# One opening and one product order of a diffusion layer: adaLN by column quarters, S5 preparation inside it, paired context matmuls

## The reference

```python
ml = split(silu(c) @ ada_w + ada_b, 9)         # shift, scale, gate x 3 sub-layers; mc likewise from c_ctx
x   = ffn_sublayer(x,   ml[0], ml[1], ml[2], ffn1_norm, w_gate, w_up, w_down)     # first feed-forward
ctx = ffn_sublayer(ctx, mc[0], mc[1], mc[2], ffn1_norm, w_gate, w_up, w_down)
# ... token mixing: S5 branch and gated linear attention branch on modulate(rms_norm(.), ml[3], ml[4])
x = x + ml[5] * y_lat
x = ffn_sublayer(x, ml[6], ml[7], ml[8], ffn2_norm, ...)                          # second one, latents only
return rms_norm(x, final_norm)

def ffn_sublayer(t, shift, scale, gate, norm_g, w_gate, w_up, w_down):
    h = rms_norm(t, norm_g) * (1 + scale) + shift
    return t + gate * (0.5 * ((silu(h @ w_gate) * (h @ w_up)) @ w_down))
```

## Time and profile before

| | |
|---|---|
| runs, device time | 1355.12, 1355.15, 1356.28 us; median 1355.15 |
| span of the profiled execution | 1354.2 us |
| busy share of the span | PE 98%, PEld 91%, DVE 64%, POOL 48%, ACT 30% |
| chain that ended last, by engine | PE 93%, DVE 3%, DMA 2%, SP's queue 1% |
| first real product of the feed-forward | 40.94 us into the span |

### The profile page before, as it was taken

How to read it: one execution, slowest core, us unless ns; L and a number is a source line. 1 busy time by engine, 2 the same in 40 slices (tenths; PEclk the granted TensorE clock), 3 DMA queues, 4 the chain that set the end, 5 groups by cost and what they waited for, 6 DMA issues and landing times.

```text
span 1354.2 us, 21460 instructions
## 1 busy us (share of the span) xinstructions
PE 1333.5 (98%) x8546; PEld 1229.7 (91%) x8546; DVE 865.3 (64%) x1376; ACT 400.0 (30%) x757; POOL 651.0 (48%) x408
## 2 busy tenths in 40 slices
PE   5999999999999999999999999999999999999998
PEld 4899999999999999998888888888998999999997
DVE  5787368568556555437656649826778765555666
ACT  4320010210210110124635321222142555544455
POOL 1544444543543533532732356636467455655554
PEclk9999999999999999999999999999999999999999
DMA  9553354353444344223322479484736233344322
GB/s 357 161 148 85 121 148 120 120 157 116 126 135 139 102 126 158 62 55 109 80 62 52 126 212 259 152 266 148 229 87 199 63 94 94 107 115 114 101 72 85
DMA packets 236782, 178.18 MB, mean 132 GB/s; under 512 B 33416, under 2 KB 211852, under 8 KB 236684
## 3 DMA queue, kind: packets, MB, share of 16 engines
q1 hardware_dynamic: 216624, 145.78, 37.6%
q10 hardware_dynamic: 20060, 31.04, 7.0%
HBM read 156.93 MB, written 19.86 MB: 131 GB/s over the span
## 4 chain that ended last, share of the span: by engine, by line
PE 93%; DVE 3%; DMA 2%; SPq 1%; issue 1%; ACT 0%; DVEq 0%; ACTq 0%
PE ps L1244 47%; PE ps L1971 13%; PE ps L1566 13%; PE ps L2030 7%; DMA ada_w<-in_ada_w_dram 2%; PE ps L1255 1%; PE ps L1844 1%; DVE ada_acc L2860 1%; DVE ps L2972 1%; PE ps L2057 1%; PE ps L1881 1%; PE ps L1669 1%; PE ps L1487 1%; PE ps L1438 1%; PE ps L1706 1%
## 5 line engine op out<-in xcount | busy, mean ns | idle before, releaser
L1143 POOL TENSOR_SCALAR w_hi<-w_raw 128x1024 fp32r<-128x1024 f32 x128 | 153.4, 1198 | 527.8 <-PE ps L1244 276.0
L1146 POOL TENSOR_TENSOR w_lo<-w_raw,w_hi 128x1024 fp32r<-128x1024 f32 x128 | 325.4, 2542 | 10.7
L1244 PE MATMUL ps<-h_hi,w_lo 128*128 128x384 f32 (+2 forms) x1000 | 291.4, 351 | 0.0
L1244 PE MATMUL ps<-h_hi,w_hi 128*128 128x384 f32 (+2 forms) x1000 | 287.1, 346 | 0.0
L1244 PE MATMUL ps<-h_lo,w_hi 128*128 128x384 f32 (+2 forms) x1000 | 287.0, 346 | 0.0
L1244 PEld LDWEIGHTS ps<-h_hi,w_lo 128*128 128x128 f32 x1000 | 178.8, 188 | 14.9 <-issue 4.3
L1244 PEld LDWEIGHTS ps<-h_lo,w_hi 128*128 128x128 f32 x1000 | 180.6, 188 | 10.5
L1244 PEld LDWEIGHTS ps<-h_hi,w_hi 128*128 128x128 f32 x1000 | 180.4, 188 | 10.7
L1222 POOL TENSOR_TENSOR w_lo<-w_raw,w_hi 128x512 fp32r<-128x512 f32 x90 | 115.6, 1297 | 105.7 <-ACT w_hi L2609 104.2
L2860 DVE SCALAR_TENSOR_TENSOR ada_acc<-ada_w,cs,ada_acc 128x1024 f32<-128x1024 f32 x70 | 108.3, 1581 | 7.8 <-DMA ada_w<-in_ada_w_dram 5.5
L1971 PE MATMUL ps<-h_hi,w_hi 128*128 128x256 f32 x360 | 102.0, 283 | 0.0
(11 more groups left out here) (459 smaller groups left out, 2635.0 us busy)
## 6 DMA issues: line engine op xcount, KB each, us to landing
w_raw<-in_ffn_w_gate_dram SPq DMA_DIRECT2D x44, 512.0 KB, 5.1
w_raw<-in_ffn_w_up_dram SPq DMA_DIRECT2D x44, 512.0 KB, 4.1
w_raw<-in_ffn_w_down_dram SPq DMA_DIRECT2D x44, 512.0 KB, 4.5
ada_w<-in_ada_w_dram ACTq DMA_DIRECT2D x32, 512.0 KB, 3.9
w_raw<-in_w_in_dram SPq DMA_DIRECT2D x32, 512.0 KB, 4.3
ada_w<-in_ada_w_dram SPq DMA_DIRECT2D x30, 512.0 KB, 4.3
c_scr<-cp ACTq DMA_DIRECT2D x16, 288.0 KB, 3.8
b_scr<-bt_sb ACTq DMA_DIRECT2D x16, 256.0 KB, 3.9
```

The source lines that it names most:

```text
L1143: pool.tensor_scalar(w_hi[:, s, 0:cols], w_raw[:, s, 0:cols], 1.0, 1.0, ALU.mult, ALU.mult)\
L1146: pool.tensor_tensor(w_lo[:, s, 0:cols], w_raw[:, s, 0:cols], w_hi[:, s, 0:cols].bitcast(F32), ALU.subtract).then_inc(w_split, 1)
L1244: last = pe.matmul(mv[2], st, mv[part], start=(first and q == 0), stop=(n == len(terms) - 1 and q == 2))
```

## The change

**Opening.** x is turned token tile by token tile. adaLN's groups 1 and 0 come in four quarters of 256 columns, 1 MB for each group and quarter in one transfer (rows of 1 KB). For each quarter PE does 8 matmuls for each group (L1324 of the changed kernel) and four of 2 columns that turn the rows (L1336, by `strip_eye`); DVE then has what it needs for k = 2q and 2q+1 of h. Quarter 0 stands before the feed-forward, quarters 1 to 3 stand between joint steps, which now are of three jobs, v=0 to 2. x times rstd is made first, and scale and shift come in one DVE instruction for latents and one for context; ACT's copy of that is `h_hi`. The loads are in the order unit 0, unit 1, quarter 0, unit 2, quarter 1, and quarters 2 and 3 when a buffer is free.

**S5 preparation.** On DVE `s5_angle` stands between quarters 0 and 1, `s5_roots` between quarters 2 and 3, and `s5_powers` behind the two first `ada_add` and ahead of the first product.

**Pairs.** The high and low parts of h and of the activations lie side by side. A k-step of the first feed-forward is five matmuls: w_hi times context high and low side by side (512 columns) into the context bank, w_lo times context high (256) into its first half, and three of 512 columns for the latents. DVE adds the two halves of the context bank (`sum_halves`) before the gate's silu and before the product; the gate's slot is given back after that. The sums for adaLN's group 2 and later stand in other banks.

```diff
-            for k in range(KD):
-                sp.dma_start(first_tile(1, k), ada_src(1, k)).then_inc(ada_here0[1][k], 16)
...
-            for k in range(KD):
-                sp.dma_start(first_tile(0, k), ada_src(0, k)).then_inc(ada_here0[0][k], 16)
...
+            first_unit(0)
+            first_unit(1)
+            quarter(0)
+            first_unit(2)
+            quarter(1)
+            sp.wait_ge(row_made, 2)
+            quarter(2)
+            sp.wait_ge(row_made, 3)
+            quarter(3)
...
+                    def pair_step(j, wh, wl, hi, lo, pair, first, final, between=None):
...
+                        mm(None, ctx_(j), wh, pair, first, False)
+                        mm(0, ctx_half(j, 0), wl, hi[:, NL:NT], False, final)
+                        mm(None, lat(j), wl, hi[:, 0:NL], first, False)
+                        mm(1, lat(j), wh, lo[:, 0:NL], False, False)
+                        return mm(2, lat(j), wh, hi[:, 0:NL], False, final)
...
+                    if joint:
+                        joint_start(0)
+                        joint_start(1)
+                        joint_step((0, 1), 0)
+                        joint_step((0, 1), 1)
+                        row_products(1, 1)
+                        row_products(1, 0)
+                        joint_start(2)
+                        joint_step((2,), 0)
+                        turn_rows(1)
+                        joint_step((2,), 1)
+                        joint_step((0,), 2)
+                        row_products(2, 1)
...
-                        act.wait_ge(job_done, (jg + 1) + i * part.jseg)
                         if n == NT:
-                            dst, src = dst.rearrange("p (b c) -> p b c", b=2), both(jg, 384)
+                            act.activation(dst[:, 0:NL], src, ACT.Silu)
+                            act.wait_ge(gate_summed, i * SEG + (part.segs * SEG + f + 1))
+                            dst, src = dst[:, NL:NT], half_sum[:, 0, :]
                         act.activation(dst, src, ACT.Silu).then_inc(slot_read[jg % 4], 1)
...
+                        if n == NT:
+                            done(jg)
+                            sum_halves(jg, 0).then_inc(gate_summed, 1)
...
-                            if f_ == 2:
-                                s5_roots()
-                            if f_ == 3:
-                                s5_powers()
...
+            s5_angle()
+            quarter_mod(1)
+            quarter_low(1)
+            quarter_mod(2)
+            quarter_low(2)
+            s5_roots()
+            quarter_mod(3)
+            quarter_low(3)
...
             for k in range(2):
                 ada_add(ADA_START, k)
-            s5_angle()
+            s5_powers()
             ffn(JOB["ffn1"], PARTS1, NT, 0, 0)
...
+            def sum_halves(j, n):
+
+                return dve.tensor_reduce(half_sum[:, n, :], ctx_(j).rearrange("p (h c) -> p c h", h=2), AX.X, ALU.add)
```

More of the change, by code:

```diff
@@ L184 @@
 STRIP = 32
-JOINT_FROM = 2
+JOINT = 3
 def ada_acc0(g):
@@ L660, in both, with tokens, ctx_half @@
         return ps[:, 2 * (j % 4):2 * (j % 4) + 2, 0:n]
[L662 to L666, removed]
+    def tokens(j):
+        return ps[:, 2 * (j % 4):2 * (j % 4) + 2, :].rearrange("p b c -> p (b c)")[:, 0:NT]
+    def ctx_half(j, part):
+        return ctx_(j)[:, NC * part:NC * part + NC]
     def ada_cols(j, c0=0):
@@ L1269, in _, with turn_vecs @@
                 last.then_inc(job_done, 1)
[L1271 to L1283, removed]
-                    if g == 0 and k < KD - 1:
-                        keep_busy(2)
+            def turn_vecs():
+                j = JOB["vec"]
+                wait_read(pe, j)
+                pe.wait_ge(vec_in, 16 * 9)
+                transpose(lat(j)[:, 0:P], vecs[:, :]).then_inc(job_done, 1)
@@ new lines, in row_products @@
+            def row_products(q, g):
+                j = JOB["open"]
+                if q or not g:
+                    pe.wait_ge(row_ok, q + (q > 0 or g == 0))
+                pe.wait_ge(ada_here0[g][q], 16)
+                for k in range(KD):
+                    r = STRIP * (k % 4)
+                    last = pe.matmul(lat(j)[r:r + STRIP, QW * g:QW * g + QW], cs_wide[:, k, :], quarter_tile(g, q)[:, k, :],
+                                     start=(k < 4), stop=(k >= 4))
+                if g == 0 or q == 0:
+                    last.then_inc(row_made, 1)
@@ new lines, in turn_rows @@
+            def turn_rows(q, groups=(1, 0)):
+                j = JOB["open"]
+                pe.wait_ge(row_ok, q + 2 - (q == 0 and groups == (1,)))
+                for g in groups:
+                    for c in range(2):
+                        at = 8 * q + 4 * g + 2 * c
+                        last = pe.matmul(ctx_(j)[:, at:at + 2], ada_row[:, q % 2, QW * g + P * c:QW * g + P * c + P], strip_eye[:, 0:2],
+                                         start=True, stop=True)
+                if q < QUARTERS - 1:
+                    last.then_inc(cols_made, 1)
+                else:
+                    last.then_inc(job_done, 1)
@@ L1479, in slot_free, with mm, pair_job @@
                         pe.wait_ge(slot_read[j % 4], j // 4 + i * (part.jseg // 4))
-                    joint = 2 if two and part.segs + i == 0 else 0
+                    def pair_step(j, wh, wl, hi, lo, pair, first, final, between=None):
+                        def mm(q, o, st, mv, start, stop):
+                            ins = pe.matmul(o, st, mv, start=start, stop=stop)
+                            if between and q is not None:
+                                between(q)
+                            return ins
+                        mm(None, ctx_(j), wh, pair, first, False)
[3 more added lines that the diff above has]
+                        return mm(2, lat(j), wh, hi[:, 0:NL], False, final)
+                    def pair_job(j, wh, wl, between=None):
+                        for k in range(KD):
+                            last = pair_step(j, wh[:, k, :], wl[:, k, :], h_hi[:, k, :], h_lo[:, k, :], h_pair[:, :, k, NL:NT], k == 0, k == KD - 1,
+                                             (lambda r: between(k, r)) if between else None)
+                        return last
+                    joint = JOINT if two and part.segs + i == 0 else 0
                     def joint_hi(v, k):
@@ L1492, in joint_lo @@
                         wh = wv((u0 + v) % 4, KD, P)[0]
-                        for q in range(2):
-                            last = pe.matmul((lat, ctx_)[q](js.gu(v))[:, 0:384], wh[:, k, :],
-                                             h_lo[:, k, 384 * q:384 * q + 384], start=False, stop=(k == KD - 1))
+                        pe.matmul(lat(js.gu(v)), wh[:, k, :], h_lo[:, k, 0:NL], start=False, stop=(k == KD - 1))
+                        last = pe.matmul(ctx_half(js.gu(v), 1), wh[:, k, :], h_lo[:, k, NL:NT], start=False, stop=(k == KD - 1))
```

423 lines of the change are left out of this document (230 added, 193 removed).

## The result

The changed kernel takes 1391.13 us (median of four runs, 1389.13 to 1392.46) against 1355.13: a ratio of 1.0261, 95% interval 1.0246 to 1.0276. It is 36 us slower, where no measurable change was forecast and 1361 was the range's upper end. Its profiled span is 1390.7 us.

A forecast was written before the change was run, and what follows sets the result against it. PE, busy 1333.5 of 1354.2 us, was taken as the bound. Terms 0 + 2.2 + 0.5 − 0.2 − 2.8 + 0.5 = +0.2 gave a span of 1354.4, written as 1355.4 us measured; range 1347.5 to 1361.

The forecast's parts named there:

- The first product starts near 25.3: Opening: the first feed-forward product starts near 25.3 us, some 15.6 us sooner than the 40.94 before.
- the end of the joint steps, 60.9: Opening: three joint jobs, with row products, turns, a wait and slow clock between, end at 60.9 us, against 66.9 before.
- the turns: Opening: turning the rows between the joint steps takes about 0.8 us in all.
- PE's lead: After the three joint jobs PE is 6.0 us ahead of the kernel before, v=3 ending at 69.2 against 75.2.
- The wait at v=4: Segment 0: s5_powers, sum_halves and silu hold v=4 until 75.2; PE waits 6.0 us, term 0 (−6.0 to +0.9).
- the forecast's upper bound: s5_powers beside POOL's splits: one DVE instruction for each POOL instruction, ending at 75.3, so v=4 starts at 76.1.
- The clock behind the wait at v=4: +0.5: Segment 0: a lower granted clock after v=4's wait costs +0.5 us (0 to 1.7).
- PE waits inside v=7: I take 2.2 (0 to 4.6): Segment 0: adaLN adds some 4 us later make v=7's sums wait, 2.2 us (0 to 4.6).
- Two reductions, a split product and a split down add some 1.4 us of DVE per tile: Side segments: DVE's added 1.4 us per tile is nearly covered by its 1.52 us of idle time.
- the term was +0.5 for all: Side segments: lost cover costs 0.1 to 0.5 us at each of five segments' ends, +0.5 us (0 to 2.5).
- Pairs: −2.8 us: Paired k-steps: 6.3 ns less each (0 to 13) over 448 steps outside v=3 to 7, −2.8 us (−6.0 to 0).
- The lock also holds the adds: Rival: adaLN adds slow too, last near 107, v=7's sums wait 5 us; +4.4, 1359.6 us; chance 0.22.

The follow-up runs named there:

- without fillers: Changed kernel without paired products, s5_powers behind the fourth product again, and 23 of 27 filler matmuls left out of the opening: 1355.20 us, ratio 0.9998.
- The run with the opening and nothing lost behind it: Changed kernel without the paired products and with s5_powers behind the fourth product of segment 0 again: 1354.77 us, ratio 0.9996 to the kernel before.
- the powers back: Changed kernel with one edit, s5_powers behind the fourth product of segment 0 again, as in the kernel before: 1379.66 us, ratio 1.0174.
- one bank: The kernel with both edits, with the context's products of every k-step but the first written into the latents' bank: 1365.98 us, one execution.
- one piece: The kernel with both edits, with the pair's 512 columns read from one SBUF piece, the latents' high part: 1359.17 us, one execution.
- the kernel with both edits: Changed kernel with s5_powers behind the fourth product again and the up job's context sum kept in PSUM: 1366.88 us, ratio 1.0083.
- the run without pairs: Changed kernel without the paired products; the new opening and s5_powers ahead of the first product stay: 1367.67 us, ratio 1.0092.
- the run with later sums: The kernel with both edits, with v=7's adaLN sums two at a place from the sixth k-step, not one from the third: 1356.21 us, ratio 1.0008.

## Why the prediction was wrong

**The opening's end: right in kind, 6 us off.** "The first product starts near 25.3" was 29.42, and the end of the joint steps, 60.9, was 66.60. The transfers were not what held the start: PE went through fillers without a gap, behind the statistics of x; without fillers the start was 27.15. Inside the joint steps, the turns were priced at 0.8 us in all and took 0.80 for each of three, from the row at 36.79 to the next product at 37.59. So PE's lead was 0.1 us at the end of v=3, not 6.0. The run with the opening and nothing lost behind it, 1354.77 us with its first product at 30.50, shows that a first product 10.4 us sooner is worth nothing here: three quarters of the row products, which stood ahead of the first product, now stand behind it on PE's path.

**The wait at v=4: the mechanism as forecast, the place late.** The chain named (powers, `sum_halves`, silu, slot) is what the rows show. Since there was no lead to eat, the 4.61 us of wait were all lost. The powers also passed more slowly: the six of 256 columns took 66.36 to 77.5, one for each POOL instruction, the forecast's upper bound. (They are 21 instructions in all, not 22, which changes 0.25 us.) Here the rule of the Trainium skill, "SBUF — State Buffer", section "Who interferes with whom", was nearer than the pace I took from narrower instructions.

**A step that failed: "The clock behind the wait at v=4: +0.5".** I priced no clock behind the wait in v=7 at all. The half clock cost about 2.4 us at v=4 (half of 79.70 to 84.50) and 8.4 in v=7, and stretches of the same length at half clock (17.49 to 17.85 us, where 9.5 is the time at full clock) came in four other kernels. Moving the sums three k-steps back, by which nothing is computed sooner, returned 10.7 us, where the wait had been 2.42.

**"PE waits inside v=7: I take 2.2 (0 to 4.6)".** 4.28 was inside, but through another door: not only the last add but the fourth gate's sum behind it. I had looked for slots that wait on DVE at v=4 and in the side segments, and not at this one.

**The step that failed most: "Two reductions, a split product and a split down add some 1.4 us of DVE per tile".** It is 0.69 + 0.69 + 0.70 + 2.15 less the old 0.96, 3.3 us, and the 1.52 us of idle time did not cover it: +11.4 in the two segments that have most adds, none in the other two, where the term was +0.5 for all. One operand moved back to PSUM returned 13.7 us, the most of any single edit. The rule on two SBUF operands (the Trainium skill, "SBUF — State Buffer", section "Who interferes with whom"), which I had cited for `s5_powers`, I did not apply to the product that the change made into one. The trace agrees with it: 2151 ns against 422 with one operand in PSUM.

**"Pairs: −2.8 us".** The mechanism was right and the term mis-sized: a k-step is 3 ns shorter, not 6.3. The two side segments without waits are 0.05 us shorter each.

**The rivals.** "The lock also holds the adds" came nearest: the last add did end after 102.3 (at 112.77). Its price was only 4.4 us: it held 5.9 of waits and 1.0 more, where 10.9 us of half clock and the slow product came on top of the waits.

## What to carry to other kernels

Before a reduction or a copy moves an operand from PSUM to SBUF, list what the instruction behind it now reads: with both operands in SBUF it ran here at the pace of a busy POOL, and most slowly right where the freed buffer lets POOL start. A wait on a PE that was full cost its length and, in all but one trace of v=7's wait, the clock behind it: price it from a stretch of the same profile at either level, and where a few small matmuls need a late result, put them as late as they can stand. An earlier start is worth only what is not moved from a waiting PE into a full one.

## What the runs showed of the chip

Behind waits of nearly one length in the same place of v=7, the granted clock fell at once and stayed at 0.50 for 17.85 us (a wait of 2.42), fell only some 2 us later (2.34 with the powers back, 2.40 in one bank), or did not fall (2.32 with one piece), with sums and matmuls of the same sizes. The run that kept its clock is one execution, and reads other data in one of five matmuls; whether that or chance decided is not shown. The four executions of the kernel with both edits all lay within 1366.1 to 1368.1 us. Of the four with the powers back alone, one took 1373.66 us at a mean granted clock of 0.994, the others 1378.92 to 1381.42 at 0.987 to 0.990.

In the stretch at half clock, matmuls of 512 columns (384 in the run without pairs) and sums of one column took turns; once at half clock, PE stayed there to the end of that stretch in every trace that shows it, while behind v=4's wait, without sums, the full clock came back after 4.8 us. The sums alone do not bring it down: PE ran them at 1.00 in the kernel before, in the run with later sums and in the one with one piece. What decides it otherwise was not tried apart.
